# Input projection and the HGRN2 scan of a hybrid trunk layer in one stage, with x spilled to DRAM

## The chip, the core and the metric

The kernel runs on one NeuronCore of a Trainium2 chip. Its time is the device time of one execution in microseconds (us), inputs and outputs in DRAM. PE is TensorE, DVE is VectorE, ACT is ScalarE, POOL is GpSimd, and SP issues nearly all DMAs. All numbers are float32. On PE a float32 matmul shows as two records in the trace.

## What is computed

Two layers of a trunk run over 640 tokens: 128 context tokens and 512 latent grid tokens, each of 1024 features. A layer mixes tokens with three parallel head groups that all read one input projection, and then runs an expert-choice mixture of experts. What matters here, from the reference:

```
h = x * (1 + sc1) + sh1
cols = h @ p['w_in']
mla_cols, hg_cols, rw_cols = _split(cols, (MLA_COLS, HG_COLS, RW_COLS))   # 672, 1280, 1152
...
# HGRN2, per direction d (forward, backward), chunked scan with a carried state:
z = clip(zf, -60, 60)
logf = log_sigmoid(z) + log1p(lb_d * exp(-z));  k = -expm1(logf);  q = silu(q)
S = decay[..., None] * S + kv          # state carried from chunk to chunk
o = o_intra + o_inter                   # inside the chunk, and from the state
...
out = o_n * silu(g)                     # o_n: rms-normed sum of both directions
# then: concat(attention, HGRN2, RWKV-7) @ w_out, DeepNorm residual with x, experts
```

So the HGRN2 scan needs only its own 1280 of the 3104 projected columns (q, values i, two gates z, output gate g), and the residual after the output projection needs x again.

## The kernel before

The kernel is a list of stages, `PHASES` (L2531), each a block of hand-written programs for the five engines. Between two stages all engines meet at a barrier, and SP, before its other work in most stages, clears the semaphores of the stage before (`e.clear_last`, L355), one instruction each. The order inside a stage is the order of the code, and semaphores join the engines. x (640 x 1024) lives in SBUF as `x_sb` for the whole run; everything else shares one buffer, `arena`. The stages of a layer are modulation (layer 0 only; for layer 1 it is inside the second normalisation), **projection**, **attention**, **HGRN2 scan**, RWKV-7, output projection with the first normalisation, routing, experts, second normalisation (`phase_norm2`, L2449).

**Projection** (`phase_project`, L483). PE transposes x (40 transposes, L519; ACT and DVE write the modulated `hT`), then runs 17 weight chunks of 128 columns ("T" groups, L524: eight matmuls over 512 tokens and eight over 128 tokens for each chunk) and 15 "tok" groups (L530: five token tiles, spans of 512, 160 and 256 columns). The eight PSUM banks go round, and ACT (L562) and DVE (L581) empty them alternately. SP loads the 17 chunks through a ring of six, and the tok weights in one 3.7 MB transfer.

**Attention** (`phase_attention`, L593). SP clears ten semaphores and loads the weights and the cache (L634); PE waits for all of that (`ld_mla`) before the key transposes (L684). POOL mixes the neighbouring tokens for RWKV-7 with `mixT` rows as scratch.

**HGRN2 scan** (`phase_hgrn`, L918). Ten units (`units`, L946) of one tile of 128 tokens and one direction each: unit u even is forward, odd is backward. For each unit:
- `levels(u)` (L965 on): some 50 short elementwise steps that build decayed queries and keys, on DVE for forward units and on POOL for backward units. DVE works one forward unit ahead: of the levels of u+2 it does 22 steps after the masks of u, and the rest after the masks of u+1. A chain wait stands behind nearly each step.
- `scores(u)` on PE (L1100, L1109), into five PSUM banks; DVE masks each bank (L1251).
- PE turns the keys (L1158), ACT copies them (L1059), PE makes the chunk's update (L1165), DVE updates the state (L1233).
- `out(u-1)` on PE (L1133, L1142, L1147), collected by DVE (L1214, L1216).

Ahead of unit 0 stand a clip of the gates (L1181), sigmoids and silus on ACT (L1043 to L1052), `prepare` (L1193, L1194) and the whole of `levels(0)` on DVE. Behind unit 9 stand a square on ACT (L1063), products with `blk` on PE (L1173, L1174), two reciprocals (L1277) and two multiplies (L1278) on DVE.

## Time and profile before

| | us |
|---|---|
| median of 3 runs | 3207.37 (3201.31 to 3212.47) |
| span of the profiled execution, first to last instruction | 3198.3 |
| PE busy | 2651.5 (83%) |
| DVE busy | 1152.6 (36%) |
| POOL busy | 754.8 (24%) |
| ACT busy | 464.6 (15%) |
| projection, layer 0, first to last of its matmuls | 50.4 to 260.4 |
| attention, layer 0 | 262.1 to 463.9 |
| HGRN2 scan, layer 0 | 464.5 to 640.2 |
| projection, layer 1 | 1631.7 to 1841.1 |
| HGRN2 scan, layer 1 | 2044.3 to 2220.3 |

The three runs lie 3.0 to 14.2 us above the profiled span. The share of a busy engine is an average over stages with different limits: the experts keep PE at 100% with the DMA engines full, the scan has PE waiting. What a change of one stage is worth has to be read in that stage: which engine the others wait for there, and what its clock was. "PEclk" in a row is the TensorE clock granted in the stretch, 1.00 being 2.4 GHz and 0.50 being 1.2 GHz.

### The profile page before, as it was taken

The page shows a single profiled execution, that of the slowest core. Times are in us where ns is not written, and L with a number is a line of the kernel's source. Part 1 is how long each engine was busy: PE and PEld are TensorE (multiplying, and loading weights), DVE is VectorE, ACT ScalarE, POOL GpSimd, SP SyncE. Part 2 cuts the span into 40 slices and gives each one's busy share as a digit, 9 for nine tenths or more (in the row PEclk, how much of TensorE's full clock was granted, in tenths as well). Part 3 has the DMA queues.
Part 4 walks back from the last instruction along what each step waited for, and adds up shares of the span by engine and source line. Part 5 has one row for each costly group of instructions (what it writes and reads, how often), then busy time and mean ns, then how long its engine had stood idle before and what let it go on. Part 6 is the DMA issues. An engine that isn't in the chain of part 4 may idle for free. (4 is left out here: it accounts for less than half of the span.)

```text
span 3198.3 us, 72152 instructions
## 1 busy us (share of the span) xinstructions
PE 2651.5 (83%) x32434; PEld 1804.7 (56%) x32434; DVE 1152.6 (36%) x2476; ACT 464.6 (15%) x957; POOL 754.8 (24%) x886
## 2 busy tenths in 40 slices
PE   6997865688784899999889978556886859999995
PEld 3564545538633666766545645455485356667672
DVE  1003668774534111111130046786745241111112
ACT  1003340042111000000020033302311010000001
POOL 0003818334213000000010055372441220000002
PEclk8999996889886999999999999878998969999997
DMA  7101000050053899999831010001400459999994
GB/s 275 53 0 39 1 10 3 1 218 4 28 203 128 323 393 396 399 392 399 307 125 40 0 39 1 10 3 60 160 30 9 204 185 379 398 391 395 396 372 140
DMA packets 73209, 552.68 MB, mean 173 GB/s; under 512 B 13848, under 2 KB 15704, under 8 KB 33992
## 3 DMA queue, kind: packets, MB, share of 16 engines
q1 hardware_dynamic: 66760, 527.11, 41.5%
q0 software_dynamic: 6144, 20.98, 2.9%
q8 instruction: 256, 4.19, 0.5%
q14 instruction: 49, 0.40, 0.0%
HBM read 523.54 MB, written 24.51 MB: 171 GB/s over the span
## 5 line engine op out<-in xcount | busy, mean ns | idle before, releaser
L2359 PEld LDWEIGHTS ps<-arena 128*64 128x64 f32 x16384 | 577.8, 138 | 90.0 <-issue 87.4
L2359 PE MATMUL ps<-arena 128*64 128x80 f32 x16384 | 598.4, 234 | 14.2 <-issue 9.6
L2373 PE MATMUL ps<-arena 128*80 128x512 f32 x1024 | 466.8, 600 | 0.0
L2434 DVE TENSOR_TENSOR arena<-arena,ps 128x160 f32<-128x160 f32 x128 | 41.1, 321 | 720.4 <-ACT arena L2394 720.4
L524 PE MATMUL ps<-arena 128*128 128x128 f32 (+1 forms) x1088 | 294.7, 434 | 4.5 <-DVE arena L577 4.5
L2373 PEld LDWEIGHTS ps<-arena 128*80 128x80 f32 x1024 | 143.9, 150 | 229.6 <-issue 218.7
L524 PEld LDWEIGHTS ps<-arena 128*128 128x128 f32 x1088 | 164.4, 191 | 134.9 <-issue 130.0
L2394 ACT ACTIVATE arena<-ps 128x160 f32<-128x160 f32 x128 | 38.8, 303 | 1006.9 <-PE ps L2359 1006.9
L2120 POOL DMA_INDIRECT sum_d<-arena x32 | 45.6, 1426 | 583.5 <-DVE arena L2426 583.5
L581 DVE COPY arena<-ps 128x128 f32<-128x128 f32 (+3 forms) x48 | 16.3, 341 | 397.7 <-PE ps L524 285.9
L2114 POOL DMA_INDIRECT arena<-h_d,arena x32 | 40.2, 1256 | 497.9 <-DVEq L2409 430.4
L2055 PE MATMUL ps<-arena 128*128 128x512 f32 x320 | 142.2, 607 | 2.1 <-PEq L1389 2.1
L1109 PE MATMUL ps<-arena 128*128 128x256 f32 x80 | 34.9, 527 | 125.6 <-DVEq L1205 125.6
L824 POOL COPY arena<-arena 32x896 f32<-32x896 f32 x2 | 1.8, 924 | 554.4 <-DVE arena L864 554.4
L530 PE MATMUL ps<-arena 128*128 128x512 f32 (+2 forms) x480 | 125.4, 423 | 0.0
L2055 PEld LDWEIGHTS ps<-arena 128*128 128x128 f32 x320 | 62.1, 195 | 81.3 <-issue 81.1
L530 PEld LDWEIGHTS ps<-arena 128*128 128x128 f32 x480 | 82.1, 189 | 42.7 <-issue 38.5
L881 DVE TENSOR_REDUCE arena<-ps 128x1 f32<-128x768 f32 (+1 forms) x80 | 65.8, 823 | 95.4 <-PE ps L716 89.0
L1544 POOL TENSOR_TENSOR arena<-arena,rwl_sb 128x512 f32<-128x512 f32 x50 | 63.6, 1279 | 107.3 <-ACT arena L1474 60.3
L1100 PEld LDWEIGHTS ps<-arena 128*128 128x128 f32 x560 | 85.8, 231 | 4.4
L1109 PEld LDWEIGHTS ps<-arena 128*128 128x128 f32 x80 | 16.0, 249 | 127.9 <-DVEq L1205 127.3
L2426 DVE SCALAR_TENSOR_TENSOR arena<-ps,arena 80x512 f32<-80x512 f32 x64 | 45.0, 742 | 112.4 <-PE ps L2373 112.4
(343 smaller groups left out, 3901.1 us busy)
## 6 DMA issues: line engine op xcount, KB each, us to landing
arena<-in_ex_w SPq DMA_DIRECT2D x128, 2048.0 KB, 15.7
arena<-in_ex_w SPq DMA_DIRECT2D x128, 1024.0 KB, 13.9
arena<-in_ada_w SPq DMA_DIRECT2D x32, 1024.0 KB, 7.8
arena<-in_w_t SPq DMA_DIRECT2D x34, 512.0 KB, 3.3
arena<-in_ada_w SPq DMA_DIRECT2D x8, 2048.0 KB, 16.0
arena<-in_w_tok SPq DMA_DIRECT2D x2, 3712.0 KB, 17.3
h_d<-x_sb SPq DMA_DIRECT2D x10, 512.0 KB, 2.6
sum_d<-x_sb SPq DMA_DIRECT2D x10, 512.0 KB, 13.5
```

Source lines behind the costliest of these rows:

```text
L524: i = nc.tensor.matmul(ps[:, n % 8, 0:c1 - c0], ring[:, a % WRING, k, :], e.hT[:, k, c0:c1], start=k == 0, stop=k == KD - 1)
L530: i = nc.tensor.matmul(ps[:, n % 8, 0:c1 - c0], e.hT[:, k, a * P:(a + 1) * P], tokw[:, k, c0:c1], start=k == 0, stop=k == KD - 1)
L881: v.link(nc.vector.reduce_max(negm[:, i:i + 1], sc[:, 0:c1 - c0], AX))
L1100: return nc.tensor.matmul(dst, keys, q_level(u, j - 1, hp), start=True, stop=True)
L1109: nc.tensor.matmul(two[:, :, 0:P], kT[:, 2 * dr + g // 2, cols], qz[:, g // 2, :, cols], start=True, stop=True)
L1544: nc.gpsimd.tensor_tensor(Mj[:, n % 4], raw[:, t], e.rwl[:, :, j + 2:j + 3, :].to_broadcast([P, 2, HH, C]), ALU.mult).then_inc(S["mj"], 1)
L2055: m = nc.tensor.matmul(ps[:, 2 * (t % 4) + n, :], e.mixT[:, k, t * P:(t + 1) * P], half, start=k == 0, stop=k == KD - 1)
L2120: e.nc.gpsimd.indirect_dma_start(e.sum_d, bass.IndirectOffsetOnAxis(ap=mem["iu"][:, x:x + 1], axis=0), mem["yR"][:, x % 2, :], None, compu ...
L2359: m = nc.tensor.matmul(gated(j)[c * 64:(c + 1) * 64, f, a, :], w13[q % WG][:, a, k, f * P + c * 64:f * P + (c + 1) * 64], xT[:, x % 2, k, ...
L2373: m = nc.tensor.matmul(rows_out(x, h), he[:, x % 2, f, :], w2[:, q % WP, f % 2, h * 512:(h + 1) * 512], start=f == 0, stop=f == KD - 1)
L2426: m = nc.vector.scalar_tensor_tensor(yR[:, x % 2, half], rows_out(x, h), gv[:, x:x + 1], g2[:, half], ALU.mult, ALU.mult)
L2434: nc.vector.tensor_tensor(he[:, b, 2 * j:2 * j + 2, :], hs[:, j % 2], gated(j)[:, :, 1, :], ALU.mult).then_inc(S["he"], 1)
```

## The change

`phase_project` and `phase_hgrn` become one stage, `phase_mix`, ahead of attention. HGRN2's own columns are projected first, the scan starts, and the other projection groups are placed between its steps on PE. One `item` is two projection groups: one token tile of the attention columns (512 and 160 columns), or one weight chunk over 512 and 128 tokens. There are sixteen items, five of attention columns, two of the output gate g and nine of RWKV-7 columns.

- Projection uses two PSUM banks instead of eight, and the masks three instead of five, so that both fit beside the scan's other banks. ACT empties all projection groups but the gates z (and the odd half of the x transposes), which DVE clips on the way out of PSUM.
- `hT` stays in use to the end, so `qz` has its own place; `levels(u)` no longer has extra buffers, and from u = 2 on it waits from its start for the scores of u-2.
- The weights of the attention and RWKV-7 columns are loaded over `x_sb` once x is transposed. x is loaded again in the attention stage (from the input, in layer 1 from a new DRAM buffer `x_d` which the second normalisation of layer 0 writes), and the first normalisation waits for that (`ld_xr`).
- One stage with its barrier and clearing goes away; the attention stage now clears the 47 semaphores of `phase_mix` instead of ten.

```diff
-WRING = 6
+WRING = 5
...
-        if u >= 4:
-            eng.wait_ge(S["at_ps"], NG * (u - 3))
+        if u >= 2:
+            eng.wait_ge(S["at_ps"], NG * (u - 1))
...
+    groups += [("q", c, 0) for c in range(2)] + [("z", c, 0) for c in range(4)] + [("v", 0, 0)]
+    groups += [("q", c, 1) for c in range(2)] + [("z", c, 1) for c in range(4)]
+    NH = len(groups)
+    groups += [("v", t, 0) for t in range(1, TILES)]
+    NV = len(groups)
+    groups += [("m", t, s) for t in range(TILES) for s in range(2)]
...
+    def pbank(n):
+
+        return n % 8 if n < NX else n % 2
...
+        return ps[:, 2 + (NG * u + g) % 3, 0:w], slice(512 * g, 512 * g + w)
...
+            if l:
+                sp.wait_ge(S["st_xd"], 16 * TILES * l)
+            sp.wait_ge(S["pj_ps"], NX)
+            sp.dma_start(w_m1, d["w_m1"][l]).then_inc(S["ld_m1"], 16)
...
+            for n in range(NH):
+                project(n)
+            scores(0)
+            turn(0)
+            evacuated(pe, NX + 6)
+            project(NH)
+            project(NH + 1)
+            chunk_state(0)
+            project(NH + 2)
+            project(NH + 3)
+            for m in range(NH, NV):
+                evacuated(pe, m)
+            item(0)
+            for u in range(1, U):
+                scores(u)
+                if units[u] not in last:
+                    turn(u)
+                item(u + (u > 1))
+                out(u - 1)
+                if units[u] not in last:
+                    chunk_state(u)
+                if u == 1:
+                    item(2)
+            item(11)
+            out(U - 1)
+            item(12)
+            item(13)
+            pe.wait_ge(S["hg_sq"], 2)
...
+            item(14)
+            item(15)
...
             prepare(0)
             for _ in run_levels(0):
                 pass
-            prepare(1)
+            for c in range(4):
+                clip(NX + 9 + c)
+                dve.wait_ge(S["pj_dve"], NX // 2 + 4 + c + 1)
+                dve.sem_inc(S["hg_z"], 1)
...
+                if u == 0:
+                    prepare(1)
...
+            sp.dma_start(e.x[:, :, :], (e.x_d if l else d["x"]).rearrange("(t p) n -> p t n", p=P)).then_inc(S["ld_xr"], 16)
...
+        dve.wait_ge(S["ld_xr"], 16 * (e.l + 1))
...
+                if more:
+                    sp.dma_start(e.x_d[t * P:(t + 1) * P, :], x[:, t, :]).then_inc(S["st_xd"], 16)
```

**On PE, inside unit 3 of the scan** (tile 4, backward). Before, the end of the scores (L1100), the turn of the keys (L1158) and the output of unit 2 (L1133, L1142) stand in a row:

```order
L1100 MATMUL ps<-arena 128x128 [waits at_sb]
L1100 MATMUL ps<-arena 128x128
L1158 MATMUL ps<-ident_sb,arena 128x128 [waits st_new]
L1158 MATMUL ps<-ident_sb,arena 128x128
L1133 MATMUL ps<-arena 128x128 [waits ld_hg,ou_sb]
L1142 MATMUL ps<-arena 64x128 [waits at_sb]
```

After, the same scores (L712), turn (L739) and output (L755, L764), in the new file's line numbers, with the attention columns of one token tile (L692, L696) between them:

```order
L712 MATMUL ps<-arena 128x128 [waits at_sb]
L712 MATMUL ps<-arena 128x128
L739 MATMUL ps<-ident_sb,arena 128x128 [waits st_new]
L739 MATMUL ps<-ident_sb,arena 128x128
L692 MATMUL ps<-x_sb,arena 128x512 [waits ld_m1,pj_act]
L692 MATMUL ps<-x_sb,arena 128x512 x7
L696 MATMUL ps<-x_sb,arena 128x160 [waits ld_m2,pj_act]
L696 MATMUL ps<-x_sb,arena 128x160 x5
L696 MATMUL ps<-arena 128x160 x2
L755 MATMUL ps<-arena 128x128 [waits ld_hg,ou_sb]
L764 MATMUL ps<-arena 64x128 [waits at_sb]
```

An item of sixteen matmuls has moved in between the turn and the output; the waits around it are the ones from before, on `st_new` (DVE's state update), `ou_sb` and `at_sb` (DVE's collection and masks), and two new ones on ACT's evacuation (`pj_act`).

**On DVE, between the levels of unit 0 and the first masks.** Before, the levels of unit 0 end with L1014, four pairs of L1193 and L1194 prepare the gates of the 512 grid tokens, and the masks (L1251) follow. The last of the pairs and what follows it:

```order
L1193 TENSOR_SCALAR arena<-arena,oml,lb_sb 128x512
L1194 TENSOR_SCALAR arena<-arena,oml 128x512
L1251 TENSOR_TENSOR arena<-ps,arena 128x512 [waits dve_chain,at_ps,hg_mask]
L1251 TENSOR_TENSOR arena<-ps,arena 128x512 [waits at_ps] x3
L1251 TENSOR_TENSOR arena<-ps,arena 128x256 [waits at_ps]
L979 COPY arena<-arena 128x256 [waits hg_q]
```

After, the last step is L611, the clips of the four gate chunks (L947) come out of PSUM and wait for PE, the masks (L1032) follow, and the preparation (L954) stands behind them:

```order
L611 TENSOR_TENSOR arena<-arena 128x256 [waits dve_chain]
L947 TENSOR_SCALAR arena<-ps 128x512 [waits dve_chain,pj_ps]
L947 TENSOR_SCALAR arena<-ps 128x512 [waits pj_dve,pj_ps] x3
L1032 TENSOR_TENSOR arena<-ps,arena 128x512 [waits pj_dve,at_ps,hg_mask]
L1032 TENSOR_TENSOR arena<-ps,arena 128x512 [waits at_ps] x3
L1032 TENSOR_TENSOR arena<-ps,arena 128x256 [waits at_ps]
L954 TENSOR_SCALAR arena<-arena,oml,lb_sb 128x512 [waits hg_e]
L955 TENSOR_SCALAR arena<-arena,oml 128x512
```

The clip of four projection groups moved behind the levels of unit 0, and the preparation of the grid tokens moved behind unit 0's masks.

**On the DMA queue (SP), at the start of the attention stage.** Before:

```order
L628 UNCONDITIONAL_BRANCH [waits barrier_Pool_Activation_PE_DVE_SP_release]
L355 ISA x10
L634 DMA arena<-in_w_uq 128x3072
L634 DMA arena<-in_w_uk 128x1024
L634 DMA arena<-in_w_uv 128x1024
L634 DMA arena<-in_c_ckv 128x2x256
```

After:

```order
L1110 UNCONDITIONAL_BRANCH [waits barrier_Pool_Activation_PE_DVE_SP_release]
L356 ISA x47
L1116 DMA arena<-in_w_uq 128x3072
L1116 DMA arena<-in_w_uk 128x1024
L1116 DMA arena<-in_w_uv 128x1024
L1116 DMA arena<-in_c_ckv 128x2x256
L1116 DMA arena<-in_c_kr 128x2x32
L1117 DMA x_sb<-in_x 128x5x1024
```

The clearing ahead of the loads (ISA) grew from 10 to 47 instructions, and the load of x stands behind the five loads that PE waits for.

## Rows read from the trace of the kernel before

**Rows 1.** busy time by stage: stretch, length, each engine, clock, DMA.

```profile
50.40:260.40 210.00, 209.88 (x784) 123.15 (x784) 8.18 (x24) 13.36 (x25) 0.00 (x0) 1.00 0.13 47
464.50:640.20 175.70, 94.81 (x1080) 85.21 (x1080) 145.13 (x343) 23.05 (x28) 104.91 (x233) 0.74 0.02 6
2044.30:2220.30 176.00, 94.31 (x1080) 84.84 (x1080) 144.47 (x343) 23.26 (x29) 105.36 (x233) 0.75 0.02 6
```

**Rows 2.** groups, projection of layer 0: busy, mean ns, idle before.

```profile
L524 PE MATMUL ps<-arena 128*128 128x128 f32 (+1 forms) x544 | 147.3, 434 | 2.1 <-DVE arena L577 2.1
...
L530 PE MATMUL ps<-arena 128*128 128x512 f32 (+2 forms) x240 | 62.7, 423 | 0.0
...
L562 ACT ACTIVATE arena<-ps 128x512 f32<-128x512 f32 (+2 forms) x25 | 13.7, 548 | 197.0 <-PE ps L524 136.5 <-PE ps L530 60.6
```

**Rows 3.** waits of the scan stage, layer 0: total us, times, longest.

```profile
PE ps L1109 <- DVEq L1205: 62.4, 5, 29.1
```

**Rows 4.** PE in order of time, units 4 and 5: start, us, idle before.

```profile
556.83 0.38 PE L1158 MATMUL ps<-ident_sb,arena 128*128 128x128 f32 x2
557.05 0.39 PE L1133 MATMUL ps<-arena 128*128 128x128 f32 x2
...
560.06 0.40 PE L1165 MATMUL ps<-arena 128*64 128x64 f32 x8
560.39 0.70 PE L1109 MATMUL ps<-arena 128*128 128x256 f32 x2
...
562.70 1.95 PE L1100 MATMUL ps<-arena 128*128 128x128 f32 x16
```

**Rows 5.** PE in order of time, the products with blk.

```profile
626.87 1.76 PE L1173 MATMUL ps<-arena,blk_sb 128*128 128x512 f32 x2 [1.91 <-ACT arena L1063]
```

**Rows 6.** DVE in order of time, scan stage of layer 0.

```profile
472.73 0.51 DVE L979 COPY arena<-arena 128x256 f32<-128x256 f32 x1 [0.22 <-DVE arena L1194]
...
491.79 0.59 DVE L1014 TENSOR_TENSOR arena<-arena 128x256 f32<-128x256 f32 x1
...
528.07 0.32 DVE L979 COPY arena<-arena 128x256 f32<-128x256 f32 x1
...
535.19 0.56 DVE L985 TENSOR_TENSOR arena<-arena 128x128 f32<-128x128 f32 x1
...
537.42 2.82 DVE L1251 TENSOR_TENSOR arena<-ps,arena 128x512 f32<-128x512 f32 x5 [0.21 <-DVE arena L1233]
540.15 0.34 DVE L985 TENSOR_TENSOR arena<-arena 128x128 f32<-128x128 f32 x1
...
549.46 0.58 DVE L1014 TENSOR_TENSOR arena<-arena 128x256 f32<-128x256 f32 x1
...
550.53 1.20 DVE L1233 SCALAR_TENSOR_TENSOR arena<-arena,ps 64x64 f32<-64x64 f32 x4
...
634.11 0.83 DVE L1278 TENSOR_TENSOR arena<-arena 128x640 f32<-128x640 f32 x1
```

**Rows 7.** POOL in order of time, its first levels.

```profile
472.70 0.40 POOL L979 COPY arena<-arena 128x256 f32<-128x256 f32 x1 [3.07 <-DVEq L1196]
...
494.55 0.79 POOL L1014 TENSOR_TENSOR arena<-arena 128x256 f32<-128x256 f32 x1
```

**Rows 8.** the page's DMA issues: count, KB each, median us to landing.

```profile
arena<-in_w_t SPq DMA_DIRECT2D x34, 512.0 KB, 3.3
...
arena<-in_w_tok SPq DMA_DIRECT2D x2, 3712.0 KB, 17.3
```

**Rows 9.** ACT, SP and PE in order of time, three stage starts.

```profile
464.49 1.28 ACT L1043 ACT_TABLE_LOAD   x1 [0.27 <-PEq L627]
...
465.97 0.34 SPq L1025 DMA_DIRECT2D arena<-in_hgf  x1
...
1852.66 0.44 PE L684 MATMUL ps<-ident_sb,arena 128*128 128x128 f32 x2 [0.43 <-DMA arena<-in_c_kr]
```

**Rows 10.** DVE in order of time, end of the second normalisation, layer 0.

```profile
1617.60 1.22 DVE L2505 TENSOR_TENSOR x_sb<-x_sb,arena 128x1024 f32<-128x1024 f32 x1
```

More of the change, by code:

```diff
@@ L491, in phase_project @@
     groups = [("x", t, h) for t in range(TILES) for h in range(2)]
     NX = len(groups)
-    groups += [("T", c, g) for c in range(NT) for g in (1, 0)]
-    groups += [("tok", t, s) for t in range(TILES) for s in range(3)]
+    groups += [("q", c, 0) for c in range(2)] + [("z", c, 0) for c in range(4)] + [("v", 0, 0)]
[3 more added lines that the diff above has]
+    NV = len(groups)
@@ new lines, in phase_mix, with evacuated @@
+    groups += [("m", t, s) for t in range(TILES) for s in range(2)]
+    NM = len(groups)
+    groups += [("g", c, s) for c in range(2) for s in (1, 0)]
+    NGT = len(groups)
+    groups += [("r", c, s) for c in range(NRW) for s in (1, 0)]
+    N = len(groups)
+    by_act = [n % 2 == 0 if g[0] == "x" else g[0] != "z" for n, g in enumerate(groups)]
+    def evacuated(eng, n):
+        own = by_act[n]
+        eng.wait_ge(S["pj_act" if own else "pj_dve"], sum(a == own for a in by_act[:n + 1]))
+    def pbank(n):
+        return n % 8 if n < NX else n % 2
@@ new lines, in chunk_state @@
+            def chunk_state(u):
+                t, dr = units[u]
+                pe.wait_ge(S["kr_sb"], u + 1)
+                for hh in range(HH):
+                    m = nc.tensor.matmul(ps[HD * (hh % 2):HD * (hh % 2) + HD, 7, 2 * P + (hh // 2) * HD:2 * P + (hh // 2 + 1) * HD],
+                                         KRt[dr][:, hh // 2, HD * (hh % 2):HD * (hh % 2) + HD],
+                                         tok[:, t, vcol + hh * HD:vcol + (hh + 1) * HD], start=True, stop=True)
+                m.then_inc(S["kv_ps"], 1)
@@ L549, in _ @@
+            item(11)
[3 more added lines that the diff above has]
+            pe.wait_ge(S["hg_sq"], 2)
+            for p in range(2):
+                nc.tensor.matmul(ps[:, 2 + 2 * p, :], e.blk[:, :], sq[:, p, 0:512], start=True, stop=True)
+                nc.tensor.matmul(ps[:, 3 + 2 * p, 0:P], e.blk[:, :], sq[:, p, 512:NTOK], start=True, stop=True
+                                 ).then_inc(S["hg_ss"], 1)
+            item(14)
+            item(15)
         @block.scalar
@@ new lines, in item @@
+            def item(n):
+                evacuate(NV + 2 * n)
+                evacuate(NV + 2 * n + 1)
+            for n in range(0, NX, 2):
+                evacuate(n)
+            evacuate(NX)
+            evacuate(NX + 1)
+            sigmoids(0)
+            evacuate(NX + 6)
+            evacuate(NX + 7)
+            evacuate(NX + 8)
+            sigmoids(1)
+            turned(0)
+            for n in range(NH, NV):
+                evacuate(n)
+            item(0)
+            for u in range(1, U):
+                if units[u] not in last:
+                    turned(u)
+                item(u + (u > 1))
+                if u == 1:
+                    item(2)
@@ new lines, in _ @@
+            item(14)
+            item(15)
+            e.done("act", a)
+        @block.gpsimd
+        def _(pool):
+            c = e.chain("pool", pool)
+            nc.gpsimd.memset(qz, 0.0).then_inc(S["hg_zero"], 1)
+            nc.gpsimd.memset(KL[0], 0.0).then_inc(S["hg_kl0"], 1)
+            c.add(nc.gpsimd.memset(KL[1], 0.0))
+            c.join()
+            k = 0
+            for u, (t, dr) in enumerate(units):
+                if dr == 0:
+                    continue
+                if k < 2:
+                    pool.wait_ge(S["hg_prep"], k + 1)
+                    pool.wait_ge(S["hg_q"], 2 * k + 2)
+                for _ in levels(nc.gpsimd, c, u):
+                    pass
+                k += 1
+                pool.sem_inc(S["lv1"], 1)
+            pool.wait_ge(S["pj_ps"], NGT)
+            for col in (0, pad_at(NPR) - 1, PAD - 1):
+                nc.gpsimd.memset(e.rwT[:, :, col:col + 1], 0.0).then_inc(S["rw_pad"], 1)
+            e.done("pool", c)
@@ L583, in _ @@
+            dve.wait_ge(S["pj_ps"], N)
+            for p in range(2):
+                nc.vector.tensor_tensor(e.mixT[:, 4 + p, :], og[:, p, :], rs[:, p, :], ALU.mult).then_inc(S["hg_on"], 1)
             e.done("dve", v)
```

802 lines of the change are left out of this document (393 added, 409 removed).

## The prediction

> **What bounds the kernel now.** I read the busy time by stage first [rows 1]. A row there has, after the stretch and its length, the busy time of PE, PEld (weight loads), DVE, ACT and POOL, then PE's granted clock, the DMA share and GB/s. The projection keeps PE busy for 209.88 of 210.00 us at clock 1.00 and uses DVE for 8 us: PE bounds it. The scan is the reverse: DVE is busy 145 of 175.7 us, PE only 94.8, and that at a mean clock of 0.74. So the two stages load different engines, and one after the other they cost 210 + 176 us a layer. The longest wait of PE in the scan says the same: its scores stand 62.4 us before DVE's signal that the levels are done, 29.1 us of it ahead of unit 0 [rows 3]. The projection's groups show no wait beyond its start [rows 2].
>
> If both fit into one stage, its length is what its fuller engine needs. PE needs the projection plus the scan's matmuls, DVE and POOL need less. So the sum is PE's, and I then ask where the scan's hand-overs hold PE up.
>
> **What goes.** The scan stage from 464.5 to 640.2 in layer 0 and from 2044.3 to 2220.3 in layer 1, each with its own entry (clips, sigmoids, the whole of the first levels, 472.73 to 492.4 [rows 6]) and its own tail: 175.7 + 176.0 = 351.7 us [rows 1]. One stage boundary is in that. The transposes of x stand in both kernels.
>
> **What comes: the scan's matmuls on PE.** The projection's matmuls are the same ones, 17 chunks (147.3 us for 544 records) and 15 groups (62.7 us for 240) [rows 2], in another order, so they stay at 210 us. The scan's are costed at full clock, since PE will be busy without a break, from units 4 and 5, which ran in a dense stretch [rows 4]:
> - scores: 560.39 to 562.70 + 1.95 = 564.65, 4.26 us, ten times: 42.6;
> - turning the keys: 556.83 to 557.05, 0.22 us, eight times: 1.8;
> - output: 557.05 to 560.06, 3.0 us, ten times: 30 (two of them leave out L1133, so this is a little high);
> - the chunk's update: 560.06 to 560.39, 0.33 us, eight times: 2.6;
> - the products with `blk`, two of 512 and two of 128 columns: 1.76 us for one of 512 [rows 5] after an idle stretch, so about 4 in all. In the projection a pair of 512 and 128 columns takes 147.3/136 = 1.08 us [rows 2], so two pairs take 2.2. Between these ends I take 2.2, PE being busy just before.
>
> Sum: 79.2 us a layer. The trace's 94.8 us of busy PE is the same work at the lower clock.
>
> **Does an item hide DVE's work?** In the middle of the scan one unit on PE is scores 4.26 + turn 0.22 + item 8.66 (147.3/17) + output 3.0 + update 0.33 = 16.5 us. A pair of units takes 33 us. On DVE a pair needs five masks twice (2.82 us), two state updates of 1.2 us, two shorter collections, and one unit's levels [rows 6]. The levels are done in two parts. The 22 steps after a forward unit's masks take 528.07 to 535.75 = 7.7 us, the rest 540.15 to 550.04 = 9.9 us [rows 6]. About 28 us in all, under 33.
>
> The order inside the pair matters more than the sum. In a backward unit DVE must end its masks (about the length of one, 0.7 to 0.9 us, behind the scores, so at 5.1 us), then the rest of the levels, and be there when the output ends, at 4.26 + 0.22 + 8.66 + 3.0 = 16.1 us. That leaves 11.0 us for a piece that took 9.9. If it is late, the state update (1.2 us, [rows 6]) and the first masks come late, and PE stops at the fourth score group, because only three banks are left for scores. On time, the first mask ends some 2.4 us after the scores begin and the fourth group begins about 3 us after: no stop. POOL's levels take 472.70 to 495.34 = 22.6 us [rows 7]. Held by the new wait they start behind the scores of u-2 and must end before those of u, 33 - 4.3 = 28.7 us later. That fits too.
>
> The first levels took 472.73 to 492.38 = 19.65 us, with POOL at its own levels all the while [rows 6, 7]; the later ones, with POOL idle for part of the time, 7.7 + 9.9 = 17.6. So POOL's company costs DVE up to 12%. Scaled so, the rest part is 11.0 us, just what is free. The Trainium skill (SBUF — State Buffer, "SBUF: two separate sides") has a rule for this: a DVE instruction with two SBUF inputs and a POOL instruction that reads SBUF exclude each other, the later one waiting for the whole of the earlier. By that rule the rest part can meet POOL at each step, since the new wait starts POOL just when DVE starts it, and forward levels are late by up to 2 us a pair; by the row they are not late. I go by the row.
>
> **Entry.** Ahead of unit 0, PE does not wait for levels: the levels of unit 0 (19.65 us) lie under the six long groups of q and z (8 x 0.86 = 6.9 us each, 41.6 us). PE may wait for weights: the first chunk is wanted 9.5 us after the issue (the transposes), then another each 1.7 us. The one large transfer landed 3.7 MB in 17.3 us [rows 8]; at that rate the six chunks land within 14 us and are wanted by 18 us. A stop of 0 to 3 us; I take 0. Two banks instead of eight: an evacuation takes ACT 0.55 us on average [rows 2], and the shortest group between two uses of a bank takes 1.7 us. A q group needs three activations and a chain wait, not in the trace; between three times 0.3 and three times 0.6 us, so PE waits 0 to 1 us twice. I take 1. One wait for the last v group: 0.6.
>
> **Hand-overs and exit.** Semaphore latencies that nothing hides, about 0.2 us at each of ten units: 2. At the end, the two multiplies into `mixT` (0.83 us each [rows 6]) now wait for the last projection group, since `mixT` and `hT` are one place: 1.7. The reciprocals, squares and roots of the tail lie under items 12 to 15 (4 x 8.66 = 35 us). Together with the entry 5.3 us a layer, with 2 and 20 as ends.
>
> **Attention.** Clearing 26 semaphores took 464.49 to 465.97 = 1.48 us, 0.057 each [rows 9]. With 37 more the loads start 2.1 us later. PE waits for them at L684 already now (0.43 us, for the cache's keys [rows 9]), so nothing covers this: +2.1, ends 1 and 3. The reload of x (2.6 MB, about 12 us at the rate above) is queued behind what PE needs and has the whole attention and RWKV-7 stage before it is read: 0. The weights of attention and RWKV-7 columns in x's place land in 3.3 us a chunk [rows 8] against 8.66 us an item: 0. The stores of x to DRAM are issued as tiles come out of the second normalisation. The last is ready at 1618.8 [rows 10], before the stage ends, and the next reader of that place waits long after: 0, at worst 3 once.
>
> **Sum.** Added per layer 79.2 + 5.3 + 2.1 = 86.6, both layers 173.2. 3198.3 - 351.7 + 173.2 = 3019.8 us for the profiled span. The median of the runs lies 9.1 us above that span, so the forecast is **3029 us**. The unknown costs alone, at their ends, give 3029 - 9 and 3029 + 38: 3020 to 3067.
>
> **Rivals.**
> - *DVE is late in the backward units.* Every pair then costs what DVE is over. With 3 us for each of four pairs it is 12 us a layer, 3053 us. For it: no more than 1 us of slack. Against: it needs levels slower than any in the trace.
> - *No real overlap.* In each unit DVE begins its levels only when PE's item is over, so a unit costs 28/2 + 8.66 = 22.7 us instead of 16.5. Nine units, two layers: +111 us, 3140 us. It would mean that the change does not do what it says. Against: the 22 steps stand right behind the masks and wait for scores alone.
> - *PE's clock falls in the merged stage.* This is the side on which it gets slower. If PE's many short stops let the granted clock drop as in the scan (0.74 [rows 1]), the 289 us of PE work take 289/0.74 = 391 us, 102 more than forecast. The stage pair before took 385.7, so the two layers end at 3029 + 203 = 3232 us. It decides at a mean clock of 289/(385.7 - 7.4) = 0.76. Against: the clock was 1.00 as soon as PE was dense, also within the scan's own dense bursts, where scores took 4.26 us. The Trainium skill (TensorE: Matmul & The Clock Gate, "A second HAM failure mode: psum-queue depth-cycling") names this very failure: small idle times of PE between groups as it goes through PSUM banks let the clock swing. [...]
> - *A little faster still.* RWKV-7 now follows attention, whose end is denser than the scan's tail, and the clocks there rise: some 5 us a layer off, 3015 us.
>
> **Chances.** Forecast (3018 to 3042) 0.66, DVE late or more stops at the entry 0.19, faster still 0.07, no overlap 0.05, clock 0.03. The range takes the first three: 3010 to 3068. About 0.3% (10 us) is what a measurement of this kernel can tell from no change. Faster by more than that 0.96, within it 0.01, slower 0.03.
>
> **What the profile after would show.** One stage of about 294 us from the first long matmul to the attention's loads, PE busy over 95% of it, clock 1.00, against 211.6 before. DVE some 50% busy with its longest waits on PE: at the clips of the grid tokens, about 20 us for unit 0, and behind the output of forward units. PE's waits inside units under 1 us each. L684's counterpart waiting 2 us more for the cache's keys. RWKV-7 to the end as before. I am wrong if PE's sum of waits in the stage is over 20 us, if scores or output are longer than 4.3 and 3.0 us beside the items, or if a later stage gives time back.

## The result and the profile after

The changed kernel takes 3007.1 us (median of four executions, 3001.1 to 3009.2) against 3204.8 us for the kernel before, run beside it: 0.938 of its time, 95% interval 0.936 to 0.940. The forecast was 3029 us with 3010 to 3068 as range. So the direction and the size of the gain came out, but the time lies 22 us below the forecast and 3 us below the range. A later series of four on another occasion gave 3009.9; the median of all eight is 3008.1. The profiled execution has a span of 3004.8 us, where the sum had 3019.8.

From the profile's page: busy time of PE, and PE's granted clock in 40 slices of the span.

```profile
span 3004.8 us, 72192 instructions
...
PE 2613.5 (87%) x32434; PEld 1773.8 (59%) x32434; DVE 1129.8 (38%) x2438; ACT 467.5 (16%) x992; POOL 761.0 (25%) x892
...
PEclk9999899999886999999999999999998789999997
```

Busy time by stretch (columns as in [rows 1]): the merged stage of layer 0 and of layer 1 from the first chunk's matmul to the last, and one unit of the scan with its item.

```profile
50.20:337.70 287.50, 286.68 (x1864) 193.88 (x1864) 140.40 (x346) 39.17 (x70) 103.08 (x233) 1.00 0.11 38
1532.50:1820.10 287.60, 286.68 (x1864) 193.88 (x1864) 140.37 (x346) 39.53 (x71) 103.06 (x233) 1.00 0.11 38
191.84:208.14 16.30, 16.30 (x146) 11.99 (x142) 11.83 (x33) 2.54 (x4) 9.77 (x21) 1.00 0.32 120
```

These answer to [rows 1]. DVE's and POOL's work is what it was (140 and 103 us), but it now lies under a PE that is busy for 286.7 of 287.5 us at clock 1.00. PE's own part of the scan cost 94.8 us of busy time at clock 0.74; here all of it and the projection's 209.9 us together are 286.7.

The same unit on PE in order of time: start, duration, line.

```profile
191.84 0.70 PE L722 MATMUL ps<-arena 128*128 128x256 f32 x2
192.38 1.50 PE L712 MATMUL ps<-arena 128*128 128x128 f32 x12
193.71 0.60 PE L722 MATMUL ps<-arena 128*128 128x256 f32 x2
194.15 1.95 PE L712 MATMUL ps<-arena 128*128 128x128 f32 x16
195.93 0.38 PE L739 MATMUL ps<-ident_sb,arena 128*128 128x128 f32 x2
196.15 8.82 PE L684 MATMUL ps<-arena 128*128 128x512 f32 x32
204.80 0.39 PE L755 MATMUL ps<-arena 128*128 128x128 f32 x2
...
207.81 0.40 PE L779 MATMUL ps<-arena 128*64 128x64 f32 x8
208.14 0.70 PE L722 MATMUL ps<-arena 128*128 128x256 f32 x2
```

Scores 191.84 to 195.93, 4.09 us; turn 0.22; item 8.65; output 3.01; update 0.33. No row of it has a wait. Note that 194.15 + 1.95 = 196.10 lies behind the next start, 195.93: the duration of the last matmul in a row reaches into the next instruction.

What PE waited for, total us, times, longest: in the merged stage of layer 0 (first fence), and from its first transposes of attention on (second).

```profile
PE ps L684 <- ACT arena L833: 2.1, 1, 2.1
PE ps L692 <- ACT arena L852: 0.8, 1, 0.8
```

```profile
PE ps L1155 <- DVE arena L1331: 8.5, 1, 8.5
PE ps L1167 <- DMA arena<-in_c_kr: 2.8, 1, 2.8
```

The 2.1 us stand ahead of the first chunk and were there before too [rows 2]. Inside the stage there is one stop of 0.8 us. The 62.4 us of [rows 3] are gone. At attention's start PE waits 8.5 us for the norms of its columns in both layers (before: 8.7 us in layer 0 and 7.2 us in layer 1), and now 2.8 and 3.0 us for the cache's keys, where layer 0 had no wait and layer 1 had 0.4 [rows 9].

### The profile page after: what moved, and what is told of

It reads as the page before. It is cut to its first block and busy times, and to the rows that moved or that the text cites. A ratio compares the mean times of both kernels' runs of the same rounds, so it can differ in the third digit from the quotient of the medians.

```text
span 3004.8 us, 72192 instructions
## 1 busy us (share of the span) xinstructions
PE 2613.5 (87%) x32434; PEld 1773.8 (59%) x32434; DVE 1129.8 (38%) x2438; ACT 467.5 (16%) x992; POOL 761.0 (25%) x892
## 5 line engine op out<-in xcount | busy, mean ns | idle before, releaser
L684 PE MATMUL ps<-arena,x_sb 128*128 128x128 f32 (+1 forms) x576 | 158.5, 434 | 0.0
L684 PE MATMUL ps<-arena 128*128 128x512 f32 (+1 forms) x512 | 139.9, 434 | 4.5 <-ACT arena L833 4.5
L684 PEld LDWEIGHTS ps<-arena,x_sb 128*128 128x128 f32 x576 | 88.0, 191 | 69.1 <-issue 68.9
L684 PEld LDWEIGHTS ps<-arena 128*128 128x128 f32 x512 | 77.7, 191 | 65.3 <-issue 60.3
L2169 PEld LDWEIGHTS ps<-arena 128*128 128x128 f32 x320 | 62.0, 195 | 81.1 <-issue 81.1
L1287 ACT ACTIVATE arena<-ps,arena 128x768 f32<-128x768 f32 (+1 forms) x80 | 63.6, 795 | 134.9 <-DVE arena L1365 112.8
L1032 DVE TENSOR_TENSOR arena<-ps,arena 128x512 f32<-128x512 f32 (+1 forms) x100 | 60.7, 634 | 61.8 <-PE ps L712 59.0
L1318 POOL TENSOR_SCALAR arena<-arena,pcol_sb 128x128 f32<-128x128 f32 x72 | 79.9, 1127 | 0.0
L1133 PE MATMUL ps<-arena 128*128 128x512 f32 (+1 forms) x192 | 59.0, 443 | 23.3 <-DVE arena L1355 23.3
L1212 PE MATMUL ps<-arena 128*64 128x64 f32 x1600 | 64.2, 226 | 16.0 <-DVE arena L1390 15.8
```

The source lines that it names most:

```text
L684: i = nc.tensor.matmul(dst[:, 0:c1 - c0], w[:, k, :], e.hT[:, k, c0:c1], start=k == 0, stop=k == KD - 1)
L1032: nc.vector.tensor_tensor(am[:, u % 2, at].rearrange("p (b n) -> p b n", b=rep), src.rearrange("p (b n) -> p b n", b=rep), hgf[:, dr:dr + ...
L1133: i = nc.tensor.matmul(ps[:, 7, 0:c1 - c0], uq[:, k, h * P:(h + 1) * P], cqT[:, k, c0:c1], start=k == 0, stop=k == 2)
L1212: m = nc.tensor.matmul(ps[c * C:(c + 1) * C, 6, (i % 2) * DV:(i % 2 + 1) * DV], pT[:, i % 2, k * P + c * C:k * P + (c + 1) * C], V[:, c0 / ...
L1287: nc.scalar.activation(pr[:, i % 2, 0:c1 - c0], sc[:, 0:c1 - c0], ACT.Exp, bias=negm[:, i:i + 1], scale=SCALE, accum_out=rsum[:, i:i + 1]) ...
L1318: c.add(nc.gpsimd.tensor_scalar(shifted[:, 1 + by, c0:c1], e.rwT[:, n, q0:q0 + c1 - c0], scale[:, n:n + 1], None, ALU.mult))
```

## Where the 15 us of span came from

Each stage's length is taken between the same instructions in both traces.

| piece | before, layers 0 / 1 | after | forecast | after minus forecast |
|---|---|---|---|---|
| first chunk to attention's first transposes, with the scan | 394.3 / 393.1 | 295.9 / 295.9 | 303.1 / 301.6 | -7.2 / -5.6 |
| attention | 195.5 / 195.5 | 199.3 / 198.6 | 197.6 / 197.6 | +1.7 / +1.0 |
| RWKV-7, first DVE step to the last transposes | 259.3 / 252.5 | 254.7 / 251.0 | 259.3 / 252.5 | -4.6 / -1.5 |
| all the rest | | | | +1.2 |

The sum is -15.0 us, the whole difference of the spans. Three places are to be explained: the merged stage (-13), RWKV-7 (-6), attention (+3). The other 7 us between 3029 and 3007 are no stage at all: the forecast added 9.1 us from span to median, and the profiled execution of the changed kernel took 3006.6 us, 1.8 above its span.

So the steps of the prediction that failed are two. Its 5.3 us a layer for entry, hand-overs and exit came to 0.6 us in layer 0 and 2.1 us in layer 1, 7.9 us too much in all. Its 9.1 us from span to median came to 1.8, 7.3 us too much. The scan's matmuls on PE (4.8 us too much in all) and RWKV-7 (6 us) are the rest, less some 4 us that attention and all other stages took more.

## Experiments

**The overlap itself.** The first question is whether the gain is the overlap at all.

```diff
-            item(0)
+            for n in range(12):
+                item(n)
             for u in range(1, U):
                 scores(u)
                 if units[u] not in last:
                     turn(u)
-                item(u + (u > 1))
                 out(u - 1)
...
-                if u == 1:
-                    item(2)
-            item(11)
             out(U - 1)
```

ACT's order follows, and SP stores the final state behind the weight loads.

> The merged stage with its code in another order: items 0 to 11 all run ahead of scores(1), and units 1 to 9 of the scan follow with no item between them. Same work, one stage, x spilled as in the changed kernel. Theory (the gain is that DVE's levels lie under PE's items): the scan's units are again as long as DVE makes them, some 14.5 us a unit from first to last as before the change against 7.6 us of PE's own work, so 60 us a layer come back, 3120 to 3135 us; and the granted clock is again near 0.75 in these units. Rival (the gain is from one stage boundary less, the shared entry and the two projection banks): under 20 us a layer come back, under 3050 us.

Measured: 3123.9 us (two executions), ratio 0.975 (0.972 to 0.977). Units 2 to 9 in that order with the first 3.7 us of item 12 behind them, by stretch, and PE's first two stops:

```profile
246.90:363.00 116.10, 81.56 (x933) 73.39 (x934) 86.01 (x217) 3.68 (x8) 73.30 (x167) 0.83 0.01 3
```

```profile
246.92 1.22 PE L722 MATMUL ps<-arena 128*128 128x256 f32 x2 [7.69 <-DVEq L960]
259.64 1.22 PE L722 MATMUL ps<-arena 128*128 128x256 f32 x2 [3.15 <-POOLq L926]
```

PE stands again 7 to 8 us for DVE's levels ahead of each forward unit and 2 to 4 us for POOL's ahead of each backward one, and attention's first transposes come at 404.8 us instead of 346.1: 58.7 us back in layer 0, in the range of the theory. PE's stops in these units sum to 42 us; the other 16 us are longer matmuls, the clock being lower between the stops. So of the 98 us that a layer wins, about 59 are the overlap of units 1 to 9 with the clock that comes with it. The remaining 39 us are a difference: the scan's entry (levels of unit 0 under the gates' groups), its tail and the boundary make it up together, and no run takes them apart. In the expectation only the clock was off: 0.83, not 0.75.

**The clock alone.** In the kernel before, PE gets filler ahead of the levels' waits:

```diff
+            filler(100)
             for u, (t, dr) in enumerate(units):
+                if u and dr == 0:
+                    pe.wait_ge(S["at_sb"], NG * (u - 1) + 1)
+                    filler(40)
                 scores(u)
```

> The kernel before, with PE kept busy in the scan stage ahead of unit 0 (100 products of 128x128 whose result is not used) and ahead of each later forward unit (40), where it stood idle for the levels. It measures what the granted clock alone is worth in the scan. Theory (small: DVE bounds the scan, the clock touches only scores and output at 1.2 GHz): the clock of the stage rises from 0.74 to over 0.9, the scan stage of 175.7 us is 5 to 12 us shorter, the kernel 10 to 24 us faster than before, 3180 to 3195. Rival (most of the merge's gain is the warm clock): over 60 us faster, under 3145 us. Second rival: the filler holds PE when the levels are done, no gain or a loss.

Measured: 3186.7 us, ratio 0.994 (0.992 to 0.996).

```profile
465.80:635.70 169.90, 143.22 (x1600) 135.19 (x1600) 145.42 (x342) 23.02 (x27) 106.22 (x233) 0.93 0.02 7
```

The clock rises to 0.93 and the scan stage takes 169.9 us instead of 175.7, 6 us a layer, in both layers. The filler itself took some of the gain back. Ahead of unit 4 DVE's levels end at 549.99, and PE, still at the filler, begins the scores 2.5 us later; ahead of unit 8 it is 1.3 us:

```profile
549.48 0.51 DVE L1014 TENSOR_TENSOR arena<-arena 128x256 f32<-128x256 f32 x1
...
552.52 0.60 PE L1109 MATMUL ps<-arena 128*128 128x256 f32 x2
```

So while DVE bounds the stage the warmer clock is worth 6 us a layer and, by an estimate that adds these two delays, some 10: a tenth of what the merge gives. The stages place 12 of the some 20 us measured; the rest is within the interval (13 to 25 us) and the wandering of RWKV-7 (below).

**DVE's slack.** The forecast gave DVE 1 us of slack in a backward unit. Two doses of extra work measure it:

```diff
                     for _ in nxt:
                         pass
+                    for _ in range(12):
+                        v.link(nc.vector.tensor_copy(Rb[0], Pb[0]))
```

> The changed kernel with 12 more copies of 128x256 on DVE, each waiting for the one before, behind the rest of the forward levels in each of units 1, 3, 5 and 7. Their results are not used. It measures DVE's slack there. The trace of the changed kernel gives 2.1 us of DVE idle ahead of the collection (units 3, 5, 7) and some 0.4 us until the fourth score group wants its bank. Theory: slack 2.5 us; with a dose d (12 times 0.3 to 0.45 us, 3.7 to 5.4) PE stops d - 2.5 = 1.2 to 2.9 us in units 3, 5 and 7, none in unit 1 which has two items, so 6 stops in the two layers: +7 to +17 us. Rival (the forecast's slack of 1 us): +16 to +26 us, with PE stops of 2.7 to 4.4 us.

Measured: 3042.0 us, ratio 0.949 (0.947 to 0.951). That is 34 us over the eight runs of the changed kernel, twice what the theory had at most and more than the rival's 26. And with nine copies:

> As the run with 12 more copies on DVE, with 9. There each copy took 0.47 us and the three stops of a layer 3.2 to 3.6 us, and behind five of the six stops PE's granted clock fell to about 0.8 for 7 to 9 us. Theory (slack of DVE 2.3 us, then one for one, and the clock's fall comes on top where the stop is long enough): dose 4.2 us, stops of 1.8 to 2.2 us, six of them, 11 to 13 us if the clock holds (3018 to 3021), up to 24 us if it falls behind these stops too (to 3031). Rival (stops cost nothing beyond their length and the 34 us of the other run came from elsewhere): the cost of this run is 0.75 of the other's, 25 us, with the clock at 1.00 behind the stops.

Measured: 3021.1 us, ratio 0.943 (0.941 to 0.944), 13 us over. PE's stops with twelve copies (layer 0 and layer 1), and the clock behind one of them:

```profile
197.60 2.49 PE L712 MATMUL ps<-arena 128*128 128x128 f32 x12 [3.23 <-DVE arena L1032]
...
1701.85 1.60 PE L712 MATMUL ps<-arena 128*128 128x128 f32 x12 [3.24 <-DVE arena L1032]
```

```profile
273.40:282.50 9.10, 9.07 (x27) 5.63 (x28) 2.28 (x4) 0.00 (x0) 4.51 (x13) 0.82 0.00 0
```

And with nine copies:

```profile
230.93 1.60 PE L712 MATMUL ps<-arena 128*128 128x128 f32 x12 [1.76 <-DVE arena L1032]
```

```profile
230.90:240.00 9.10, 9.07 (x35) 5.25 (x36) 8.70 (x25) 0.73 (x2) 5.64 (x12) 1.00 0.01 2
```

Twelve copies took 5.62 us and PE stopped six times for 3.2 to 3.6 us; nine took 3.78 us and it stopped six times for 1.4 to 1.8 us. Both say the same slack: 2.0 to 2.4 us. From there on a delay costs one for one, behind units 3, 5 and 7 alone, as unit 1 has two items. The second reading is the price of a stop. Behind the short ones the clock stayed at 1.00, and a layer's stage grew by 5.7 us for 4.9 us of stops. Behind five of the six longer ones its mean was 0.81 to 0.83 over the next 9 us (the same twelve matmuls took 2.49 us, against 1.60 where it held). A mean of 0.82 over 9.1 us is, by estimate, 3.3 us at 1.2 GHz, which costs 1.6 us. Layer 0 grew by 15.6 us for 10.1 us of stops. Of the 5.5 us beyond the stops 0.8 stood behind the three short ones too, which leaves 1.6 us for each of its three falls. Layer 1, with two falls, grew by 13.3 us for 9.7. Both layers' stages give 29 us of the 34; the other 5 are the RWKV-7 stages of that execution (261.5 and 249.6 us). The rival that stops cost only their length is refuted: it had 25 us for nine copies, and they cost 13. What stops between 1.8 and 3.2 us do, no run shows.

**POOL beside DVE.** POOL makes the levels of units 1 and 3 only.

> The changed kernel without POOL's levels for units 5, 7 and 9 (left out, so their scores use the levels of unit 3): POOL is idle while DVE makes the forward levels of units 6 and 8. Theory (POOL at its levels makes DVE's slower, as in the changed kernel's trace, where the 22 steps took 7.85 us with POOL busy and 5.4 us with POOL idle): all heads take 5.4 us and the rest of the levels about 7 us instead of 9.7. Rival (the forecast's 12% for POOL's company): rest of the levels 8.7 us or more. PE bounds the stage, so its length stays the same within 1 us either way: 3005 us.

Measured: 3004.7 us, one execution, within the changed kernel's own spread. The 22 steps with POOL idle, the same with POOL busy, and the rest of the levels, in the changed kernel:

```profile
164.03:169.44 5.41, 5.41 (x14) 2.42 (x13) 5.03 (x23) 0.11 (x1) 0.00 (x0) 1.00 0.00 0
196.62:204.47 7.85, 7.85 (x30) 4.26 (x28) 7.47 (x23) 1.99 (x3) 5.53 (x10) 1.00 0.13 54
179.93:189.67 9.74, 9.74 (x59) 6.03 (x59) 9.12 (x25) 1.01 (x3) 9.01 (x20) 1.00 0.01 2
```

The rest of the levels with POOL idle, in the experiment, and DVE's next wait:

```profile
180.40:187.60 7.20, 7.20 (x22) 3.61 (x21) 6.57 (x25) 0.71 (x2) 0.00 (x0) 1.00 0.00 0
```

```profile
192.25 0.42 DVE L980 COPY arena<-ps 128x256 f32<-128x256 f32 x1 [4.67 <-PE ps L769]
```

The 22 steps ahead of unit 6 take 5.4 us in the experiment too, each short step on two operands of 128x128 its 0.29 us. So POOL's company costs DVE 45% in the first part (7.85 against 5.41 us) and 35% in the second (9.74 against 7.20), not the 12% that the forecast took. The stage is no shorter without it, since PE bounds it. The Trainium skill (SBUF — State Buffer, "SBUF: two separate sides") says that of a DVE instruction with two SBUF inputs and a POOL instruction that reads SBUF the later waits for the whole of the earlier. The runs agree with it in direction; that each wait is as long as POOL's instruction, they don't show (23 steps grew by 2.4 us together).

**Attention's start.** The loads go out ahead of the clearing:

```diff
-            e.clear_last(sp)
             for dst, src in ((uq, d["w_uq"][l]), (uk, d["w_uk"][l]), (uv, d["w_uv"][l]),
...
                 sp.dma_start(dst, src).then_inc(S["ld_mla"], 16)
+            e.clear_last(sp)
```

> The changed kernel, with the five loads of attention's weights and cache issued ahead of the clearing of the 47 semaphores instead of behind it. Theory (the clears are what holds the loads up): they are issued some 2.7 us earlier, PE's wait for the cache's keys falls from 2.8 us to under 0.5 us in each layer, and the span falls by 5 us, 3004.8 to about 3000. Rival (the reload of x, 2.6 MB, issued right behind them, takes the DMA engines from them): the wait stays at 2 us or more though the issue is earlier.

Measured: 3003.5 us, ratio 0.937 (0.936 to 0.939); span 3001.3. The first load on SP and PE's wait, in the changed kernel and then in the experiment (layer 0, and for PE layer 1 too):

```profile
342.33 0.33 SPq L1116 DMA_DIRECT2D arena<-in_w_uq  x1
...
352.36 0.44 PE L1167 MATMUL ps<-ident_sb,arena 128*128 128x128 f32 x2 [2.75 <-DMA arena<-in_c_kr]
```

```profile
339.20 0.33 SPq L1115 DMA_DIRECT2D arena<-in_w_uq  x1
...
350.05 0.44 PE L1167 MATMUL ps<-ident_sb,arena 128*128 128x128 f32 x2 [1.01 <-DMA arena<-in_c_kr]
...
1830.22 0.44 PE L1167 MATMUL ps<-ident_sb,arena 128*128 128x128 f32 x2 [0.17 <-DMA arena<-in_c_kr]
```

The load goes out 2.7 us earlier against attention's first transposes (345.72 here, 346.14 there), and the wait falls from 2.75 to 1.0 us in layer 0 and from 2.97 to 0.2 us in layer 1. The reload of x stands further behind the loads here too, but that isn't the reason: the wait stays when most of the reload goes (next experiment). So the clears are the cause of the wait, as the theory has it, though in layer 0 it stayed above the 0.5 us expected. Only layer 1 kept the gain: its attention took 195.7 us instead of 198.6. In layer 0 it took 199.4 against 199.3, as the clock was at 0.91 and 0.95 from 370 to 420 us, where the changed kernel had 1.00. The span is 3.5 us shorter instead of 5, and the two intervals of the ratio overlap.

**The spill of x.** No stores, no wait for them, a fifth of the reload:

```diff
-                    sp.dma_start(e.x_d[t * P:(t + 1) * P, :], x[:, t, :]).then_inc(S["st_xd"], 16)
...
-            sp.dma_start(e.x[:, :, :], (e.x_d if l else d["x"]).rearrange("(t p) n -> p t n", p=P)).then_inc(S["ld_xr"], 16)
+            sp.dma_start(e.x[:, 0, :], d["x"][0:P, :]).then_inc(S["ld_xr"], 16)
```

> The changed kernel with no stores of x to DRAM, no wait for them, and a reload of the first token tile alone (0.5 MB instead of 2.6 MB); the residual sum then adds what stands in x's place, which changes values and no instruction. It measures what the spill costs. Theory (it costs nothing: the stores end under the expert stage's end, the reload is behind what PE waits for and long before its reader): the same within 0.2% of the changed kernel run beside it, PE's waits at attention's start for the cache's keys still 2.7 to 3 us. Rival (the reload takes DMA from attention's loads, or the five stores hold up the second normalisation): 3 us or more faster, with the wait for the cache's keys at 2 us or less.

> The changed kernel once more, for a second profile and for a comparison beside the run without the spill. Merged stage as in the first profile, within 0.5 us (287.5 us from the first chunk's matmul to the last); the RWKV-7 stages anywhere from 250 to 258 us, which sets how far the span differs from 3004.8: by up to 5 us. If the RWKV-7 stages are within 1 us of the first profile's 254.7 and 251.0, the difference to the kernel before would be the order of the stages after all and not the wandering clock.

Measured: 3006.9 us (0.9385, 0.937 to 0.940) without the spill, 3009.9 (0.9402, 0.939 to 0.942) with it. The medians differ by the 3 us that the rival asked for, but the intervals overlap. Its other sign is absent: the wait at attention's start stands almost unchanged without most of the reload, 2.65 us in layer 0 and 3.19 in layer 1:

```profile
352.24 0.44 PE L1165 MATMUL ps<-ident_sb,arena 128*128 128x128 f32 x2 [2.65 <-DMA arena<-in_c_kr]
```

From RWKV-7's last transposes in layer 0 to the next layer's first chunk, with the stores in it, it takes 731.2 us with them and 730.5 without. So the spill costs nothing that can be seen; 3 us are within the noise.

In this second profile of the changed kernel the merged stage took 287.5 us again in layer 0, but 289.1 us in layer 1, where 288.1 was the most expected: the clock's mean was 0.83 over its first 10 us.

**RWKV-7.** The rival "a little faster still" said that this stage gains some 5 us behind attention. The kernel before, once more:

> The kernel before, once more, for a second profile: how long its RWKV-7 stage is. In the first profile 259.3 and 252.5 us; in the changed kernel and four variants of it 249.6 to 261.5, mean 253.4, with mean clocks of 0.88 to 0.94. Theory (the stage's length wanders with the granted clock in either kernel; only the one table load of 1.3 us and some 1 us of clock at its start belong to the new neighbour): here 250 to 256 us in each layer. Rival (RWKV-7 behind the scan is slower by 4 to 5 us than behind attention): again 257 us or more in layer 0 and 252 or more in layer 1.

Measured: one execution, 3203.6 us; its RWKV-7 stages took 256.0 and 252.4 us, at the theory's upper edge in layer 0 and by the rival's second number in layer 1, so this run alone decides nothing. The stage by stretch, first where it was slowest (twelve copies, layer 0), then the second profile of the changed kernel:

```profile
560.60:822.10 261.50, 203.05 (x3730) 154.66 (x3730) 157.78 (x244) 69.23 (x131) 88.31 (x80) 0.88 0.21 77
```

```profile
545.50:795.50 250.00, 192.61 (x3729) 149.03 (x3729) 155.21 (x244) 69.24 (x131) 88.15 (x80) 0.93 0.21 81
2024.40:2274.90 250.50, 194.33 (x3730) 149.45 (x3730) 156.32 (x244) 69.22 (x131) 88.35 (x80) 0.92 0.22 80
```

In 18 such stages with RWKV-7 behind attention it took 249.6 to 261.5 us, 253.0 in the mean; in six with RWKV-7 behind the scan (both profiles of the kernel before and the run with filler) 252.4 to 259.3, 255.5 in the mean. DVE's work in it is the same each time; PE's busy time goes up as its mean clock goes down. Fixed in it is one table load of ACT (1.28 us), which stands at the stage's start only behind the scan. The difference of the means, 2.4 us, is less than the spread of one order. So the 6 us of the two profiles are mostly which execution was profiled; whether 1 us a layer beyond the table load belongs to the new order stays open. Attention wanders too: in the second profile of the kernel before it took 201.6 us in layer 0, at a mean clock of 0.94, against 195.5 in the first. (At 5 us a layer the rival would come to 3019 us, not to the 3015 that it names.)

**A faster version.** At attention's start PE waits for its columns' statistics and for the loads, though the columns are complete after item 4. Both move into the merged stage:

```diff
+            token_squares(0)
+            token_squares(1)
             item(12)
+            for t in range(2, TILES):
+                token_squares(t)
+            a.add(nc.scalar.activation(mst[:, 0:TILES], mst[:, 0:TILES], ACT.Sqrt, bias=e.eps[:, 0:1], scale=1.0 / QR))
...
+            sp.wait_ge(S["hg_o"], 1)
+            for dst, src in ((cache[:, :, 0:KVR], d["c_ckv"][l].rearrange("(t p) n -> p t n", p=P)),
```

> A version meant to be faster than the changed kernel: the statistics and the scaling of attention's query and key columns (ACT's squares and roots, DVE's reciprocal and ten multiplies) and the five loads of attention's weights and cache are moved from attention's start into the merged stage, under items 12 to 15. The columns are complete after item 4. Theory (what PE waits for at attention's start is only this chain, 8.5 us to its first transposes, and the loads, 2.8 us): PE's first transposes come some 2 us after the last item, with no wait for the cache's keys; 6.5 + 2.8 = 9 us a layer, 2987 to 2990 us. Rival (ACT and DVE have no room under the last items: ACT's ten squares come between evacuations, PE has two banks only): PE stops of 1 to 3 us in items 12 to 15, or the last two multiplies come late, and over a third of it is lost, above 2993 us.

Measured: 2990.4 us (five executions, 2983.6 to 2992.2), ratio 0.932 (0.930 to 0.934).

```profile
338.71 1.56 DVE L1098 TENSOR_TENSOR arena<-arena 128x640 f32<-128x640 f32 x2 [9.29 <-PE ps L700]
```

```profile
340.59 3.39 PE L1186 MATMUL ps<-ident_sb,arena 128*128 128x128 f32 x15 [1.99 <-PEq L629]
```

The first transposes of attention come 2.0 us behind the last item instead of 8.5, no wait for the cache's keys is left, and DVE still stood 9.3 us idle before its last two multiplies, so its new work had room. PE has no stop in items 12 to 15, so nothing speaks for the rival: the kernel is 17 us faster than the changed one, at the theory's edge.

## The prediction, step by step

- **What goes, 351.7 us:** right. **The projection's matmuls stay at 210 us:** right.
- **Scan matmuls on PE, 79.2 us:** 287.5 us less the one stop of 0.8 and the projection's 209.9 leave 76.8. Two readings failed. The scores were taken to the end of the last matmul's duration (562.70 + 1.95 [rows 4]), which reaches 0.17 us into the next instruction; start to start they are 4.09 us, ten times 0.17. And the outputs of units 0 and 1, which leave out one pair of products, take 2.1 us instead of 3.0; the prediction saw that and left it in. The products with `blk` took the 2.2 us forecast (318.05 to 320.22). The pieces put right sum to 75.8; where the last 1.0 us lies, the rows don't say.
- **Entry, hand-overs and exit, 5.3 us:** the term that was sized worst, and the first of the two failed steps. Of the 1.6 us at the entry 0.8 came. Of the 2 us of semaphore latencies none came: no row between units shows a wait. At the exit DVE's multiplies did come behind the last item and hold up the next stage, but only by 1.1 us: ACT begins attention's squares 1.9 us behind its last evacuation, before 0.9. And in layer 0 a table load that stood in this chain before has gone; the merged stage's own roots have their table load at 318.54, ahead of items 14 and 15. In layer 1 no such load stood there before. ACT at attention's start, first after, then before, both of layer 0:

```profile
337.72 0.28 ACT L850 ACTIVATE arena<-ps 128x128 f32<-128x128 f32 x1 [1.18 <-PE ps L684]
...
339.66 0.52 ACT L1251 ACTIVATE arena<-arena 128x384 f32<-128x384 f32 x1 [1.66 <-PEq L618]
```

```profile
260.36 0.38 ACT L562 ACTIVATE arena<-ps 128x256 f32<-128x256 f32 x1 [5.04 <-PE ps L530]
261.25 0.52 ACT L768 ACTIVATE arena<-arena 128x384 f32<-128x384 f32 x1 [0.50 <-ACTq L496]
...
266.46 1.28 ACT L771 ACT_TABLE_LOAD   x1
```

  So from the last item to attention's first transposes it takes 8.45 us in layer 0, before 8.61, and in layer 1 PE's wait there grew from 7.18 to 8.46. The whole term was 0.6 us in layer 0 (0.8 - 0.2) and 2.1 us in layer 1 (0.8 + 1.3). The lower end given for it, 2, lay above the one and at the other: no reason stood there why the hand-overs could not be nothing, or why a stage's start could not lose something too. That the table load (1.28 us) would go was no part of the forecast; with it the term would have been 1.9 us in layer 0 too. (The upper end is added wrongly too: entry to exit, attention and stores give 34 us, not the 38 in the prediction.)
- **DVE in time in the backward units:** right, with more room than said. The rest of the levels took 9.74 us, not 11.0. The scaling for POOL's company was put on a piece that already had it; this row of the kernel before, not read then, shows POOL busy for 8.93 of its 9.89 us:

```profile
540.15:550.04 9.89, 2.36 (x42) 2.06 (x40) 9.27 (x25) 0.00 (x0) 8.93 (x20) 0.67 0.00 0
```

  The window was longer as well: from 179.93 to DVE's collection at 191.75 are 11.8 us, as items of the attention columns take 9.04 us (179.46 to 188.50) and not 8.66. So the slack was 2.0 to 2.4 us, as the doses show, instead of 1, and the rival "DVE late" (0.19), which pulled the range up to 3068, had less for it than it seemed. The 12% itself was wrong too, the company costs 35 to 45%; but a duration that was measured in company wants no factor at all.
- **Attention +2.1 us:** 3.8 and 3.1. The mechanism was right, the size short. SP's first load came 4.6 us behind the last item instead of 1.7: 2.1 us by the 37 clears, as forecast, and 0.8 by the later end of the stage, which the sum did not carry over to the loads. In layer 0 the first 12 records of the products that follow the key transposes also took 8.16 us instead of 7.12, at a mean clock of 0.66 instead of 0.76.
- **x reload and stores, 0:** right, by the run without them.
- **RWKV-7 to the end as before:** within what the stage wanders by itself, 12 us. The range held nothing for that.
- **Clock at 1.00:** right. The Trainium skill (TensorE: Matmul & The Clock Gate, "A second HAM failure mode: psum-queue depth-cycling") warned of small idle times as banks go round; with two banks PE's stops in the stage were 0.8 us together, and the clock's mean was 1.00 over it. So the failure that the page tells of does not show here. With the twelve copies, which stopped PE for 3.2 to 3.6 us at a time, the clock did fall.
- **+9.1 from span to median:** the second of the two, 7 us. In all eleven kernels profiled since, the profiled execution took 1.8 to 2.2 us more than its own span. So some 2 us of the 9.1 belong to the kernel, and 7 were the distance of that one execution from the median of three, a draw. With +2 the forecast would have been 3021.8, and its lower end 3003.

In sum, the span was 15 us shorter than forecast (13 the stage, 6 RWKV-7, mostly its wandering, 3 and 1 the other way), and 7 us were the step from span to median. The theory of the gain stands: PE's items cover DVE's levels. Its sizes failed, and a few microseconds of RWKV-7 or attention the other way would have brought the time into the range without making them right.

## What to carry to other kernels

Two stages bound by different engines can merge at the price of the fuller engine. Here that engine's sum could be read almost without an addition for hand-overs; that holds as long as its own queue never runs dry and the other engine has a microsecond or two of slack in each unit. Measure that slack with doses of dead work: one gives the threshold, two the slope, and the slope may be steeper than one where stops become long enough to cost the clock. After a merge, look at the next stage's first wait: what it waits for is often complete much earlier and can be done under the merged stage (17 us here, for no new work).

## What the runs showed of the hardware

- A stop of PE of 1.4 to 1.8 us in a stretch at clock 1.00 left the clock there, six times of six. A stop of 3.2 to 3.6 us was followed five times of six by a mean of 0.81 to 0.83 over the next 9 us. In layer 0, with three falls, the stage grew by 5.5 us more than its stops, and by 0.8 us more with three short stops and no fall.
- Elementwise steps of DVE on SBUF beside a busy POOL: 7.85 us against 5.41, and 9.74 against 7.20. Single steps on 128x128 operands took 0.29 us with POOL idle and 0.30 to 0.58 us beside it.
- The same RWKV-7 stage, the same instructions, took 249.6 to 261.5 us from one execution to another, with PE's mean clock between 0.94 and 0.88. Attention took 195.5 and 201.6 us in the two profiles of the kernel before (layer 0, clock 0.94 in the longer). One profile of each kernel cannot tell 5 us of such a stage from chance.
